# A hybrid encoder layer on one core: the rests of split weights used last, and the closing loads issued ahead

## What is computed

```python
h = rms_norm(x) * (1 + sc1) + sh1
gate_b, gate_c, x_conv, q, k, v, g_conv, g_attn = split(h @ w_in)
y_conv = (gate_b * causal_conv(gate_c * x_conv, w_conv)) @ w_conv_out
y_attn = attention(rope(q), rope(k), v, sinks) @ w_attn_o
x = x + g1 * ((sigmoid(g_conv) * y_conv + sigmoid(g_attn) * y_attn) @ w_mix_out)
h = rms_norm(x) * (1 + sc2) + sh2
ffn = swiglu(h, shared) + sum of the 8 of 64 experts that route(h) picks, each a swiglu
y = rms_norm(x + g2 * ffn) * final_gain
```

## Time and profile before

| | us |
|---|---|
| median of three runs | 2250.11 |
| lowest and highest | 2250.03, 2259.94 |
| profiled execution, its own time | 2247.8 |
| its span, first to last instruction | 2246.0 |
| PE busy (share of the span) | 2140.7 (95%) |
| DVE busy | 1230.8 (55%) |
| ACT busy | 1007.1 (45%) |
| POOL busy | 459.5 (20%) |
| mean granted clock of TensorE | 0.979 |

### The profile page before, as it was taken

How to read it: one execution, slowest core, us unless ns; L and a number is a source line. 1 busy time by engine, 2 the same in 40 slices (tenths; PEclk the granted TensorE clock), 3 DMA queues, 4 the chain that set the end, 5 groups by cost and what they waited for, 6 DMA issues and landing times. The chain is left out here.

```text
span 2246.0 us, 41415 instructions
## 1 busy us (share of the span) xinstructions
PE 2140.7 (95%) x11538; PEld 1834.9 (82%) x11539; DVE 1230.8 (55%) x2000; ACT 1007.1 (45%) x1773; POOL 459.5 (20%) x549
## 2 busy tenths in 40 slices
PE   5999899999999989998988999999999999999995
PEld 2767559999999989997878788888888888888862
DVE  4623673112332331215777787688677778678636
ACT  3403793211011121113432676677676677667622
POOL 1400000000000000000000444434444444434335
PEclk8999899999999999999999999999999999999998
DMA  7360501112111101116322899899889899989758
GB/s 294 125 241 9 177 1 56 38 47 66 47 47 40 34 19 47 47 52 233 115 64 86 295 326 312 252 304 335 278 285 340 279 325 309 312 253 324 253 133 244
DMA packets 153532, 395.59 MB, mean 176 GB/s; under 512 B 22124, under 2 KB 90932, under 8 KB 128900
## 3 DMA queue, kind: packets, MB, share of 16 engines
q1 hardware_dynamic: 122260, 311.61, 38.5%
q0 software_dynamic: 31040, 82.51, 14.9%
q10 hardware_dynamic: 176, 0.75, 0.1%
HBM read 353.93 MB, written 74.53 MB: 191 GB/s over the span
## 5 line engine op out<-in xcount | busy, mean ns | idle before, releaser
L2098 PE MATMUL ex_pgu<-ex_wgu_hi,ex_xT_hi 128*128 (+1 forms) x784 | 314.9, 402 | 9.9 <-DVE ex_xT_lo L2268 9.2
L2256 DVE TENSOR_TENSOR ex_wgu_lo<-ex_stage_gu,ex_wgu_hi (+1 forms) x252 | 291.8, 1221 | 37.2 <-ACT ex_wgu_hi L2175 37.0
L2098 PE MATMUL ex_pgu<-ex_wgu_hi,ex_xT_lo 128*128 (+1 forms) x784 | 308.1, 393 | 0.0
L2098 PE MATMUL ex_pgu<-ex_wgu_lo,ex_xT_hi 128*128 (+1 forms) x784 | 307.2, 392 | 0.0
L2175 ACT CAST ex_wgu_hi<-ex_stage_gu (+1 forms) x252 | 245.7, 1047 | 35.6 <-issue 18.7
L983 PE MATMUL cv_ph<-fourth_r,cv_split 128*128 128x352 f32 (+1 forms) x1152 | 222.0, 328 | 2.1 <-DVE cv_split L1029 2.1
L983 PEld LDWEIGHTS cv_ph<-fourth_r,cv_split 128*128 128x128 f32 x1152 | 196.0, 189 | 2.2 <-DVE cv_split L1029 2.2
L1624 POOL MEMSET ex_rows<- 128x1088 f32 x1 | 1.0, 1004 | 951.6 <-ACT third_r L1596 951.6
L2098 PEld LDWEIGHTS ex_pgu<-ex_wgu_hi,ex_xT_hi 128*128 128x128 f32 x784 | 148.4, 189 | 41.4 <-issue 11.8
L2098 PEld LDWEIGHTS ex_pgu<-ex_wgu_hi,ex_xT_lo 128*128 128x128 f32 x784 | 147.5, 188 | 31.4
L2098 PEld LDWEIGHTS ex_pgu<-ex_wgu_lo,ex_xT_hi 128*128 128x128 f32 x784 | 147.9, 189 | 28.7
(11 more groups left out here) (355 smaller groups left out, 4245.1 us busy)
## 6 DMA issues: line engine op xcount, KB each, us to landing
ex_stage_gu<-in_w_exp_gate SPq DMA_DIRECT2D x64, 1024.0 KB, 8.8
ex_stage_gu<-in_w_exp_up SPq DMA_DIRECT2D x64, 1024.0 KB, 11.7
ex_stage_dn<-in_w_exp_down SPq DMA_DIRECT2D x64, 1024.0 KB, 8.4
front_room<-in_w_ada SPq DMA_DIRECT2D x26, 512.0 KB, 5.8
w_ahead<-in_w_in SPq DMA_DIRECT2D x24, 512.0 KB, 3.8
third<-in_w_ada SPq DMA_DIRECT2D x16, 512.0 KB, 8.6
early_late<-in_w_in SPq DMA_DIRECT2D x16, 512.0 KB, 3.9
front_room<-in_w_in SPq DMA_DIRECT2D x3, 2048.0 KB, 12.6
```

The source lines that it names most:

```text
L2098: last = pe.matmul(pgu[:, :], xT[a][:, k, :], w, start=(k == 0 and (a, c) == PASSES[0]), stop=(k == KT - 1 and (a, c) == PASSES[-1]))
L2256: dve.tensor_tensor(gu_piece(1, slot, q), gu_raw(slot, q), gu_piece(0, slot, q).bitcast(F32), ALU.subtract).then_inc(gu_lo, 1)
```

## The change

Two edits. In the two branches, the convolution and mixing the passes of an output get a new order: for k = 0 to 7 the two passes with rounded weights, then for k = 0 to 7 the pass with the rests of the weights. PE waits for the rounded weights at the start and for the rests before the seventeenth round. In mixing, tile 0 waits for the rounded weights slice by slice, then for the rests slice by slice, and `m_lo` is waited for at the second round.

At the close SP loads x2 of all eight tiles at once, without a wait for PE, then waits itself for the landing of the last even scatter, and loads the nine tiles of even sums one behind another. `even_stored` is gone.

```diff
+ROUNDS = [(k, 0, x) for k in range(KT) for x in range(2)] + [(k, 1, 0) for k in range(KT)]
...
@@ conv_branch, PE @@
-                                pe.wait_ge(w_lo, i * 6 + (jj + 1))
-                                for k in range(KT):
-                                    for pw, px in PASSES:
-                                        for c, (a, b) in enumerate(THIRDS):
-                                            last = pe.matmul(ph[jj % 2][:, c, 0:b - a], wp[jj % 3][pw][:, k, :], h[px][:, k, a:b],
...
+                                pe.wait_ge(w_hi, i * 6 + (jj + 1))
+                                for k, pw, px in ROUNDS:
+                                    if (k, pw) == (0, 1):
+                                        pe.wait_ge(w_lo, i * 6 + (jj + 1))
+                                    for c, (a, b) in enumerate(THIRDS):
+                                        last = pe.matmul(ph[jj % 2][:, c, 0:b - a], wp[jj % 3][pw][:, k, :], h[px][:, k, a:b],
...
@@ branch, PE @@
-                            pe.wait_ge(w_lo, i * 2 + (o + 1))
-                            for k in range(KT):
-                                if o:
+                            pe.wait_ge(w_hi, i * 2 + (o + 1))
+                            for k, pw, px in ROUNDS:
+                                if (k, pw) == (0, 1):
+                                    pe.wait_ge(w_lo, i * 2 + (o + 1))
+                                if o and (pw, px) == (0, 0):
                                     pe.wait_ge(x_lo_done, k + 1)
...
@@ mix_and_route, PE @@
-                        pe.wait_ge(m_lo, t + 1)
-                        for k in range(KT):
-                            if t == 0:
+                        pe.wait_ge(m_hi, t + 1)
+                        for k, pw, px in ROUNDS:
+                            if t == 0 and (pw, px) == (0, 0):
+                                pe.wait_ge(w_hi, k + 1)
+                            if (k, pw, px) == (0, 0, 1):
+                                pe.wait_ge(m_lo, t + 1)
+                            if t == 0 and pw:
                                 pe.wait_ge(w_lo, k + 1)
...
@@ experts, SP @@
-                    AHEAD = 3
-                    for t in range(AHEAD):
+                    for t in range(NT - 1):
                         x2_rows(t)
-                    for t in range(AHEAD, AHEAD + 2):
-                        sp.wait_ge(tail_sum, t - AHEAD + 1)
-                        x2_rows(t)
-                    sp.wait_ge(even_stored, 1)
+                    sp.wait_ge(y_stored[0], pairs_of(sp) * 16 + 16)
                     for t in range(NT):
                         R = rows_of(t)
                         sp.dma_start(sums[t][:R, :], self.sum_rows[0][t * P:t * P + R, :]).then_inc(sum_loaded[t], 16)
-                        if AHEAD + 2 + t < NT - 1:
-                            x2_rows(AHEAD + 2 + t)
...
@@ experts, POOL @@
-                    wait(y_stored[0], m * 16 + 16)
-                    pool.sem_inc(even_stored, 1)
                     wait(y_stored[1], m * 16 + 16)
```

More of the change, by code:

```diff
@@ L911, in conv_branch @@
         h = (self.h_hi, self.h_lo)
-        PASSES = ((0, 0), (0, 1), (1, 0))
         with ExitStack() as st:
@@ L978, in _ @@
                                 pe.wait_ge(sem, i * 2 + (n + credit))
-                                pe.wait_ge(w_lo, i * 6 + (jj + 1))
-                                for k in range(KT):
-                                    for pw, px in PASSES:
-                                        for c, (a, b) in enumerate(THIRDS):
-                                            last = pe.matmul(ph[jj % 2][:, c, 0:b - a], wp[jj % 3][pw][:, k, :], h[px][:, k, a:b],
-                                                             start=(k == 0 and (pw, px) == PASSES[0]),
-                                                             stop=(k == KT - 1 and (pw, px) == PASSES[-1]))
+                                pe.wait_ge(w_hi, i * 6 + (jj + 1))
[4 more added lines that the diff above has]
+                                        last = pe.matmul(ph[jj % 2][:, c, 0:b - a], wp[jj % 3][pw][:, k, :], h[px][:, k, a:b],
+                                                         start=(k, pw, px) == ROUNDS[0], stop=(k, pw, px) == ROUNDS[-1])
                                 last.then_inc(job, 1)
@@ L1166, in _ @@
                             pe.wait_ge(read, i + 1)
-                            pe.wait_ge(w_lo, i * 2 + (o + 1))
-                            for k in range(KT):
-                                if o:
-                                    pe.wait_ge(x_lo_done, k + 1)
-                                for pw, px in PASSES:
-                                    for c, (a, b) in enumerate(THIRDS):
-                                        last = pe.matmul(ph[o][:, c, 0:b - a], wp[o][pw][:, k, :], v[px][:, k, a:b],
-                                                         start=(k == 0 and (pw, px) == PASSES[0]),
-                                                         stop=(k == KT - 1 and (pw, px) == PASSES[-1]))
+                            pe.wait_ge(w_hi, i * 2 + (o + 1))
[3 more added lines that the diff above has]
+                                if o and (pw, px) == (0, 0):
+                                    pe.wait_ge(x_lo_done, k + 1)
+                                for c, (a, b) in enumerate(THIRDS):
+                                    last = pe.matmul(ph[o][:, c, 0:b - a], wp[o][pw][:, k, :], v[px][:, k, a:b],
+                                                     start=(k, pw, px) == ROUNDS[0], stop=(k, pw, px) == ROUNDS[-1])
                             last.then_inc(job, 1)
@@ L1430, in mix @@
                             pe.wait_ge(x2_done, t - 1)
-                        pe.wait_ge(m_lo, t + 1)
-                        for k in range(KT):
-                            if t == 0:
-                                pe.wait_ge(w_lo, k + 1)
-                            for px, pw in PASSES:
-                                for h in range(2):
-                                    last = pe.matmul(pm[t % 2][:R, h, :], m_split[px][:, t % 2, k, 0:R], w_split[pw][:, k, h * 512:(h + 1) * 512],
-                                                     start=(k == 0 and (px, pw) == PASSES[0]),
-                                                     stop=(k == KT - 1 and (px, pw) == PASSES[-1]))
+                        pe.wait_ge(m_hi, t + 1)
[5 more added lines that the diff above has]
+                            if t == 0 and pw:
+                                pe.wait_ge(w_lo, k + 1)
+                            for h in range(2):
+                                last = pe.matmul(pm[t % 2][:R, h, :], m_split[px][:, t % 2, k, 0:R], w_split[pw][:, k, h * 512:(h + 1) * 512],
+                                                 start=(k, pw, px) == ROUNDS[0], stop=(k, pw, px) == ROUNDS[-1])
                         last.then_inc(mixed, 1)
@@ L1835, in experts @@
         w_loaded = self.first_w
-        filled, ahead, even_stored = S("ex_filled"), S("cb_ahead"), S("cb_even_stored")
+        filled, ahead = S("ex_filled"), S("cb_ahead")
         x2_loaded = [S(f"cb_x2_{t}") for t in range(NT - 1)]
```

## The result

The changed kernel takes 2243.32 us, median of eight runs (2236.61 to 2245.71), against 2250.15 us for the kernel before in eight runs beside it. The ratio is 0.9963, interval 0.9947 to 0.9978. The forecast was 2227.4 us with a range from 2218 to 2240: the kernel is faster, but by 6.8 us and not by 22.7. The profiled execution took 2241.32 us around a span of 2239.5.

A forecast was written before the change was run, and what follows sets the result against it. TensorE, busy 95% of the span, was taken as the bound, with a close of transfers, POOL and DVE. Starts and clock 9.2 us plus end 13.5 made 22.7 us, taking 2250.1 to 2227.4 us, range 2218 to 2240.

The forecast's parts named there:

- the change at the end: Close: earlier x2 and sums loads, POOL's end gains 10.4 us and DVE's catching up 3.1, together 13.5 us.
- The bounds of the close: Close: the gain of 13.5 us was given bounds of 5 and 17 us.
- The first accumulating load: Close: POOL's first accumulating load goes out at 2178.9, not 2189.3 us, 10.4 us earlier.
- POOL's first product: Close: POOL multiplies first at 2188.2 instead of 2202.3 us, some 14 us earlier.
- The starts: Branches, convolution, mixing: PE starts on ACT's rounded copy alone, 1.2 to 1.6 us earlier each, 5.2 us in all.
- The clock: After the four start gaps: less time at 1.2 GHz gives back 4.0 us, of at most 7.8.
- The last blocks: Rival: x2 loads collide with the last gathers and scatters, 2.5 us for each of two blocks; 2232 us, 12%.
- The order of the rounds: Rival: in branches, convolution and mixing the new order itself costs, 2272 us at 10 ns a product; 4%.
- DMA: Rival: transfers bound the end, so only the x2 loads taken out and the starts count; 2240 us, 12%.
- All comes back: Rival: clock nearly whole (13 us) and DVE keeping up at the close (17 us); 2220 us, 15%.
- the starts give nothing: Rival: another wait ends at the starts, so only the end counts; 2236.6 us, 7%.
- The signs: Right: shorter PE waits, full attention-branch clock, earlier sums and POOL product. Wrong: late accumulating loads, ACT scatter wait, pitch over 0.17 us.

The follow-up runs named there:

- e6: e3 with one load of sums ahead of the last odd scatter and eight behind its landing; 2226.87 us, ratio 0.9894.
- e3: The changed kernel, with POOL's product of tile t also waiting for DVE's output of tile t - 3; 2228.89 us, ratio 0.9893.
- e5: The changed kernel, with DVE's sum written back to PSUM and read there by the square and output product; 2232.72 us, ratio 0.9915.
- e12: The changed kernel, with POOL waiting for its own product of tile t - 1 before it goes on; 2228.74 us, ratio 0.989.
- e1: The kernel before with only the change's order of the rounds, its close as before; 2246.62 us, ratio 0.9981.
- e9: The changed kernel with a copy of one column behind each of POOL's products at the close; 2244.84 us, ratio 0.9976.
- e10: The changed kernel, but sums loaded behind PE's second closing tile and even_stored, as before; x2 loads still ahead; 2246.0 us, ratio 0.9974.

## Why the prediction was wrong

**The step that failed** is in the change at the end: "With POOL paced at 3.97 us a tile against 2.67 us of product, DVE gets a gap each tile", and before it "I keep this step". Neither part held. The 3.97 us were not a property of the accumulating loads, but of these loads with loads of even sums landing between them, one to one; e6, with such loads between and no x2, has POOL's products 3.8 us apart too. In the change the last of the sums landed at 2185.3 us, and the accumulating loads landed from 2186.48 to 2206.03 us, (2206.03 - 2186.48) / 8 = 2.44 us apart. POOL takes 0.6 us for an issue and 2.3 for a product, 2.9 us, so it became the slower of the two, its products lay back to back, and DVE got no gap at all. The very thing named as the cause of the 8.19 us, products of POOL back to back, was carried to the new schedule only as the middle between a DVE that kept up "wholly" and "not at all", with 13.9 us behind POOL as the worst case. The measured 27.7 us are worse. The path through PE was wrong as well: "five more end near 2219.5 us, before POOL" let PE's closing tiles run without a stop, but PE needs DVE to empty PSUM, stood 13.35 us, and its last three tiles set the end. In the terms of the sum: counted from the last even scatter, POOL's end gained 62.0 - 47.4 = 14.7 us instead of 10.4, and the part behind it lost 27.7 - 13.9 = 13.8 us instead of gaining 3.1; that leaves 0.9 of 13.5.

**The bounds of the close**, 5 to 17 us, missed the 0.9 for the same reason: both ends assumed that DVE lags as far behind POOL as it did or less. No rival was made of the lock. The Trainium skill's page SBUF — State Buffer, section Who interferes with whom, gives the rule that was cited, that whichever starts first has the ports for the whole instruction while the other blocks; e3 to e5 agree with that (1.28 us against 19.38 with one operand more in SBUF). By this page of the Trainium skill alone the output product would be held for the rest of one product, 2.3 us at most. The runs show that only where POOL stands still between two: the longest hold in e12 is 3.22 - 1.28 = 1.9 us; in the change it was 18.1 us. The prediction's "the 8.19 us agree" was a misreading already, as 8.19 - 1.28 = 6.9 us is more than the 2.67 us of one product.

**The first load of sums** was forecast to leave 8.4 us sooner after the even scatter; it left 13.8 - 5.1 = 8.7 us sooner. **The first accumulating load** was to gain 10.4 us and gained 5.8 in that measure (19.2 to 13.5): nine loads of sums issued beside the last odd scatter made POOL wait 6.81 us for it, a wait that wasn't forecast. e6 shows that its removal is worth 0.6 us. **POOL's first product** gained 32.2 - 22.1 = 10.1 us against the 14.1 that were forecast in this measure: the fourth load's block was gone as said, but the first addition was issued 4.6 us later than forecast (10.4 - 5.8) and landed in 8.5 us instead of 9.3.

**The starts** were right. The time from the first cast to PE's first product fell by 1.25 to 1.27 us at the attention branch, the second branch and the convolution and by 1.46 at mixing, against 1.2, 1.2, 1.2 and 1.6: 5.2 us as forecast.

**The clock** was mis-sized, 1.8 us (7.0 less 5.2) instead of 4.0. The attention branch kept its clock, as forecast, for 1.6 us, but with some luck: e1 and e9 have the same program up to there and fell at this branch, and not at the convolution. The convolution didn't, with 0.85 us of idle time instead of 2.11 before its first product; its 1.7 us stayed away. The second branch gave 0.8. From mixing's first product to the first expert product the changed kernel took 0.5 us longer, not shorter; so the two gaps that stayed long gave 0.3 us together instead of 0.7.

**The rivals.** The last blocks didn't collide: 933.9 and 934.0 us in front of the last even scatter. The order of the rounds costs nothing: the attention branch's 1152 products take 189.71 us at full clock against 191.26 with the fall. DMA was not the bound at the end, although that rival's 2240 us came nearest: the additions landed at 2206 us, 33 us before the end. "All comes back" had DVE keeping up, which e12 shows to take one more wait. That the starts give nothing is ruled out by the waits above.

**The signs.** None of the three signs of being wrong appeared, and those of being right came or nearly so. They watched SP, POOL's loads and PE's starts, and none watched DVE's output product or PE's closing tiles, where the time went.

## What to carry to other kernels

When work on POOL is brought closer together, ask what a DVE instruction with two SBUF operands beside it will do: it may be passed over until POOL stands still, so count POOL's idle moments, not its busy share. A wait of POOL for its own last instruction cut the hold from 18.1 to under 2 us here; one operand moved to PSUM took it away. A spacing read from a trace belongs to the mix of transfers that it was read from; when the change thins out the mix, work it out anew, and see which engine is the next bound.

## What the runs showed of the hardware that was not expected

- A DVE product with both operands in SBUF, 1.28 us by itself, lasted 19.38 us, through seven products of POOL. The issue of a DMA between two (0.6 us) and a one-column copy (0.14 us) didn't let it in; a wait of POOL for its own semaphore did, each time, with POOL idle for 0.30 us or, in the last tiles of e12, for less than 0.1.
- A POOL product's record grows while its queue is full (2.34, 2.65, and 3.88 us in e9, with starts 2.4 us apart), so its start-to-start time is the one to go by.
- The last odd scatter held POOL for 6.81 us with nine loads issued beside it, and for 2.70 us with one.
- The same program showed its fall of the clock at different starts: the order of the rounds of the change falls at convolution, second branch and mixing in its own profile (3.4, 3.4 and 6.8 us), and at attention branch, second branch and mixing in e1's (3.4, 6.8 and 3.4 us); the total was 13.6 us in both, against 20.4 us before. e10, with the same program in these stages, has 17.0 us (3.4, 6.8 and 6.8).
